# Expert rows gathered in quarters and turned by VectorE in 32x32 blocks, instead of turned by TensorE

## The reference

```python
xf = rms_norm(h, w)                       # (1024, 1024)
logits = xf @ router_w + router_b         # 32 experts
top_logit, top_idx = lax.top_k(logits, 4)
gate = jax.nn.softmax(top_logit, axis=-1)
...
gu = x_blk @ w_gate_up[e] + b_gate_up[e]  # (rows, 2048)
g = jnp.minimum(gu[:, :1024], 7.0)
u = jnp.clip(gu[:, 1024:], -7.0, 7.0)
act = (u + 1.0) * (g * jax.nn.sigmoid(1.702 * g))
yb = act @ w_down[e] + b_down[e]          # added at the rows' tokens, times the gate
```

## Time and profile before

| | |
|---|---|
| median of 3 runs | 2207.5 us (2200.51 to 2211.68) |
| profiled execution | 2205.89 us, span 2204.2 us, mean granted clock 0.989 |
| busy over the span | PE 2130.6 us (97%), PEld 1655.0 (75%), DVE 1569.1 (71%), ACT 1324.6 (60%), POOL 581.7 (26%) |
| experts stage | from 832.31 us (first product) to the end |

### The profile page before, as it was taken

How to read it: one execution, slowest core, us unless ns; L and a number is a source line. 1 busy time by engine, 2 the same in 40 slices (tenths; PEclk the granted TensorE clock), 3 DMA queues, 4 the chain that set the end, 5 groups by cost and what they waited for, 6 DMA issues and landing times.

```text
span 2204.2 us, 38936 instructions
## 1 busy us (share of the span) xinstructions
PE 2130.6 (97%) x13778; PEld 1655.0 (75%) x13779; DVE 1569.1 (71%) x1479; ACT 1324.6 (60%) x1496; POOL 581.7 (26%) x556
## 2 busy tenths in 40 slices
PE   7989999999999989999999999999999999999997
PEld 7867777777777766777777777877887777777775
DVE  4165767676576457787787787787987777767776
ACT  4266666757454225576676675776876566565665
POOL 1120101010075343153353331232331222122222
PEclk9999999999999988999999999999999999999999
DMA  4101212121256539899899898999998898887993
GB/s 153 36 23 47 68 37 69 36 62 56 82 193 199 178 126 357 302 327 347 312 338 350 313 343 283 373 348 345 390 374 314 283 317 327 297 307 266 331 327 112
DMA packets 267125, 515.15 MB, mean 234 GB/s; under 512 B 34821, under 2 KB 77264, under 8 KB 267052
## 3 DMA queue, kind: packets, MB, share of 16 engines
q1 hardware_dynamic: 243052, 471.90, 59.5%
q0 software_dynamic: 17088, 39.14, 7.0%
q10 hardware_dynamic: 6912, 3.15, 0.5%
HBM read 475.82 MB, written 42.45 MB: 235 GB/s over the span
## 4 chain that ended last, share of the span: by engine, by line
PE 59%; SPq 1%; DMA 1%; issue 1%; DVE 0%; ACT 0%; POOL 0%; ACTq 0%; POOLq 0%; DVEq 0%
PE ex_gu L2431 31%; PE ex_yp L2475 15%; PE ex_rest L2453 6%; PE ex_rest L2492 3%; PE ex_gu L2383 1%; SPq L1360 1%; PE ex_tr L2391 1%; PE ex_gu L2391 1%; DMA ex_bias<-bp_s 1%; PE ex_gu L2418 0%; PE ex_tr L2383 0%; PE ex_yp L2422 0%; DVE ex_wlo L2302 0%; ACT ex_whi L2027 0%; PE ex_rest L2447 0%
## 5 line engine op out<-in xcount | busy, mean ns | idle before, releaser
L2302 DVE TENSOR_TENSOR ex_wlo<-ex_raw,ex_whi 128x2048 fp32r<-128x2048 f32 x387 | 873.9, 2291 | 216.5 <-ACT ex_whi L2027 187.3
L2027 ACT ACTIVATE ex_whi<-ex_raw 128x2048 fp32r<-128x2048 f32 x387 | 733.9, 1927 | 176.5 <-PE ex_gu L2431 126.1
L2431 PE MATMUL ex_gu<-ex_whi,ex_xhi 128*128 128x512 f32 x1024 | 284.6, 400 | 1.0 <-DVE ex_xlo L2341 1.0
L2431 PE MATMUL ex_gu<-ex_whi,ex_xlo 128*128 128x512 f32 x1024 | 274.9, 390 | 0.0
L2431 PE MATMUL ex_gu<-ex_wlo,ex_xhi 128*128 128x512 f32 x1024 | 274.9, 390 | 0.0
L2431 PEld LDWEIGHTS ex_gu<-ex_whi,ex_xhi 128*128 128x128 f32 x1024 | 186.8, 189 | 57.1 <-issue 20.6
L2431 PEld LDWEIGHTS ex_gu<-ex_whi,ex_xlo 128*128 128x128 f32 x1024 | 192.8, 188 | 41.1
L2431 PEld LDWEIGHTS ex_gu<-ex_wlo,ex_xhi 128*128 128x128 f32 x1024 | 192.8, 188 | 40.7
L57 PE MATMUL at_job<-xnT_hi,at_whi 128*128 128x512 f32 x416 | 178.4, 429 | 5.3 <-DVE at_nxt_qa L777 2.9
L59 PE MATMUL at_job<-xnT_hi,at_wlo 128*128 128x512 f32 x416 | 164.2, 395 | 0.0
L58 PE MATMUL at_job<-xnT_lo,at_whi 128*128 128x512 f32 x416 | 163.4, 393 | 0.0
(11 more groups left out here) (379 smaller groups left out, 3563.5 us busy)
## 6 DMA issues: line engine op xcount, KB each, us to landing
ex_raw<-in_w_gate_up_dram SPq DMA_DIRECT2D x512, 512.0 KB
ex_raw<-in_w_down_dram SPq DMA_DIRECT2D x256, 512.0 KB
at_raw<-in_w_in_dram SPq DMA_DIRECT2D x25, 512.0 KB
gT<-at_gst SPq DMA_DIRECT2D x32, 256.0 KB, 2.4
mg_g<-gT SPq DMA_DIRECT2D x32, 256.0 KB, 3.8
raw_o<-in_w_out_dram SPq DMA_DIRECT2D x8, 512.0 KB, 5.7
op_x<-in_x_dram SPq DMA_DIRECT2D x8, 512.0 KB, 4.0
out_dram<-op_h SPq DMA_DIRECT2D x8, 512.0 KB, 2.9
```

What stands on the lines that cost most here:

```text
L2027: nc.scalar.activation(w_hi[:, i % RING, :], raw[:, i % SLABS, :], ACT.Copy).then_inc(hi_d, 1)
L2302: nc.vector.tensor_tensor(w_lo[:, slot, :], raw[:, i % SLABS, :], w_hi[:, slot, :].bitcast(F32), ALU.subtract).then_inc(lo_d, 1)
L2431: mm = nc.tensor.matmul(gu[:, half, h, :], x[:, k, :], w[:, kk, h, :], start=half == 0 and k == 0 and n == 0, stop=k == KD - 1 and n == 2)
```

## The change

The normalized rows are stored in `xn_s` with their columns permuted: four quarters of 256 values, of which quarter q holds of each group of 128 columns the 32 columns q*32 to q*32+31. Five indirect DMAs fetch 128 quarters each (4 for the block's 128 rows, 1 for the rest's 32). So partition 32*q+i of piece a holds quarter q of row 32*a+i, and a transpose in 32x32 blocks, which VectorE has, gives the transposed tile. VectorE does this in three instructions in each block, into the hidden tile's buffer (`x_t`), half the columns ahead of the hidden's second lo part together with the rest, half behind it. ScalarE's hi copies and VectorE's lo subtractions read this buffer in place of PSUM; ScalarE's copy of the rest goes. `turn_x` leaves TensorE's queue, which then waits for x by `take_x` as before. The table of tokens gets a form in quarters (`rows_of`), for which TensorE turns 16 small pieces at the stage's start, and VectorE and GpSimd do some more small steps. `normalize` is four instructions in place of one. For blocks not in the table on the chip, GpSimd loads the numbers with 25 DMAs in place of 5 (this happens twice, at the end). The weights' loads keep their order.

```diff
@@ normalize, in output_and_route
-                    nc.vector.scalar_tensor_tensor(out=xn[:, s, :], in0=ht[:, s, :], scalar=rstd[:, t:t + 1],
-                                                   in1=wB[:, :], op0=ALU.mult, op1=ALU.mult).then_inc(xn_done, 1)
+                    piece = lambda b, q: b.rearrange("p (k q c) -> p q k c", k=KD, q=Q)[:, q, :, :]
+                    for q in range(Q):
+                        last = nc.vector.scalar_tensor_tensor(
+                            out=xn[:, s, q * XW:(q + 1) * XW].rearrange("p (k c) -> p k c", k=KD), in0=piece(ht[:, s, :], q),
+                            scalar=rstd[:, t:t + 1], in1=piece(wB[:, :], q), op0=ALU.mult, op1=ALU.mult)
+                    last.then_inc(xn_done, 1)
@@ SyncE, start of experts
-            sp.wait_ge(x_in, 32)
+            for s, n in landed:
+                sp.wait_ge(s, n)
             load(4, 0)
@@ ScalarE, take_x
-                    act.wait_ge(raw_mm, SLABS * (b - 1) + 8)
-                for g in range(3):
-                    act.wait_ge(x_tr, 3 * b + g + 1)
-                    if g < 2:
-                        dst, src = x_hi[:, 4 * g:4 * g + 4, :], gu[:, 0, g, :].rearrange("p (k c) -> p k c", k=4)
-                    else:
-                        dst = x_rest[:, :, :].rearrange("p (q h) c -> p h q c", h=2)
-                        src = tr[:, 0:2 * P].rearrange("p (h q c) -> p h q c", h=2, q=Q)
-                    nc.scalar.activation(dst, src, ACT.Copy).then_inc(xh_d, 1)
+                for g in range(2):
+                    mine = slice(4 * g, 4 * g + 4)
+                    act.wait_ge(x_tr, 2 if isinstance(b, int) and b == 0 else 3 * b + 1 + 2 * g)
+                    nc.scalar.activation(x_hi[:, mine, :], x_t[:, mine, :], ACT.Copy).then_inc(xh_d, 1)
@@ GpSimd, load_slots and gather
+                    for a in range(NQ):
+                        pool.dma_start(nxt_q[q * CAP2:(q + 1) * CAP2, a, :],
+                                       slots[bass.ds(b * CAP + a * CAP2, CAP2), :]).then_inc(idx_in, 16)
...
-            def gather():
-                pool.indirect_dma_start(out=xg[:, :], out_offset=None, in_=xn_s[:, :],
-                                        in_offset=bass.IndirectOffsetOnAxis(ap=nxt[:, 0, 0:1].bitcast(U32), axis=0))\
-                    .then_inc(x_in, 16)
-                pool.indirect_dma_start(out=xg2[:, :], out_offset=None, in_=xn_s.rearrange("t (q c) -> (t q) c", q=Q),
-                                        in_offset=bass.IndirectOffsetOnAxis(ap=idx2[:, 0:1], axis=0)).then_inc(x_in, 16)
+            def gather(table):
+                for a in range(NQ):
+                    pool.indirect_dma_start(out=xg[:, a, :], out_offset=None, in_=xn_s.rearrange("t (q c) -> (t q) c", q=Q),
+                                            in_offset=bass.IndirectOffsetOnAxis(ap=table(a), axis=0)).then_inc(x_in[max(a - 1, 0)], 16)
@@ VectorE
+            def turn_x(b, g):
+                if g == 0:
+                    for s, n in landed:
+                        dve.wait_ge(s, n * (b + 1))
+                after(dve, h_tr, 3 * b + g - 2)
+                mine = slice(4 * g, 4 * g + 4)
+                nc.vector.transpose(x_t[:, mine, :].rearrange("p k (a c) -> p k a c", a=Q),
+                                    pieces[:, mine, 0:Q, :]).then_inc(x_tr, 1)
+
+            def turn_x_rest(b):
+                if not isinstance(b, int) or b > 0:
+                    dve.wait_ge(raw_mm, SLABS * (b - 1) + 8)
+                nc.vector.transpose(x_rest[:, :, :], pieces[:, :, Q, :]).then_inc(x_tr, 1)
...
                 split_lo(b, 11)
+                turn_x(b + 1, 0)
+                turn_x_rest(b + 1)
                 hidden_lo(b, 1)
+                turn_x(b + 1, 1)
                 take_x(b + 1)
@@ VectorE, start of experts
+            for a in range(Q):
+                dve.wait_ge(*landed[max(a - 1, 0)])
+                last = nc.vector.transpose(x_t[:, :, a * CAP2:(a + 1) * CAP2], pieces[:, :, a, :])
+            last.then_inc(x_tr, 2)
             take_x(0)
+            dve.wait_ge(*landed[Q - 1])
+            turn_x_rest(0)
@@ TensorE
                 if more:
                     turn_hidden_rest(b)
-                turn_x(b + 1)
                 main(10)
...
+            for a in range(Q):
+                for q in range(Q):
+                    last = nc.tensor.matmul(turned_q[q * CAP2:(q + 1) * CAP2, a, :], rt["table"][:, a * CAP2:(a + 1) * CAP2],
+                                            rt["pair_sum"][:, 0:NE], start=True, stop=True)
             last.then_inc(t_tr, 1)
-            pe.wait_ge(tab_d, 2)
-            turn_x(0)
```

More of the change, by code:

```diff
@@ L1894, in experts @@
         one_col = sb("ex_one", [P, 1])
-        over_n, cum, base1 = (sb(f"ex_{n}", [P, NE]) for n in ("over", "cum", "base1"))
-        home, low, destf = (sb(f"ex_{n}", [P, NT * TOPK]) for n in ("home", "low", "destf"))
+        over_n, cum, base1, home, low, destf = (rt["table"][:, n * NE:(n + 1) * NE] for n in range(6))
         tabf = sb("ex_tabf", [1, MAXOVER + 1])
@@ L1939, in experts @@
         y_ev, y2_ev = sem("e_y_ev"), sem("e_y2_ev")
-        idx_in, idx2_d, x_in, y_out = sem("idx_in"), sem("idx2_d"), sem("x_in"), sem("e_y_out")
-        mid_d, cur_d, piece_d = sem("e_mid"), sem("e_cur"), sem("e_piece")
+        idx_in, idx_d, x_in, y_out = sem("idx_in"), sem("idx_d"), [sem(f"x_in{n}") for n in range(NQ - 1)], sem("e_y_out")
+        landed = [(x_in[n], 32 if n == 0 else 16) for n in range(NQ - 1)]
+        cur_d = sem("e_cur")
         ones_d, bias_in = sem("e_ones"), [sem(f"e_bias_in{n}") for n in range(2)]
@@ L2155, in next_rows @@
             def next_rows(b, on_chip=True):
-                if not isinstance(b, int) or b > 0:
-                    hold(pool, x_in, 32 * b, spare)
-                    nc.gpsimd.tensor_copy(mid[:, :, :], nxt[:, :, :]).then_inc(mid_d, 1)
-                    hold(pool, mid_d, b, spare)
+                for s, n in landed:
+                    hold(pool, s, n * b, spare)
+                nc.gpsimd.tensor_copy(mid[:, :, :], nxt[:, :, :]).then_inc(idx_d, 1)
+                hold(pool, idx_d, 3 * b - 2, spare)
                 if on_chip:
@@ L2166, in next_rows @@
                     load_slots(b)
-                    hold(pool, idx_in, 16 * (1 + Q) * (b - NE + 1), spare)
-                rows()
-                hold(pool, idx2_d, b + 1, spare)
-                if not isinstance(b, int) or b > 0:
-                    hold(pool, x_tr, 3 * b, spare)
-                gather()
+                    hold(pool, idx_in, 16 * (1 + Q * (1 + NQ)) * (b - NE + 1), spare)
+                    nc.gpsimd.tensor_scalar(idx[:, :], nxt_q[:, :, 0].bitcast(U32), float(Q), quarter[:, 0:1],
+                                            ALU.mult, ALU.add).then_inc(idx_d, 1)
+                hold(pool, idx_d, 3 * b - 1, spare)
+                hold(pool, x_tr, 3 * b, spare)
+                gather(lambda a: idx[:, a:a + 1])
             def first_rows():
@@ L2217, in body @@
                     scatter(t)
-                hold(pool, piece_d, b + 1, spare)
+                hold(pool, idx_d, 3 * b + 3, spare)
                 if isinstance(b, int) and b == NE - 2:
@@ L2374, in _ @@
             pe.sem_inc(slab_mm, RING)
-            def turn_x(b):
-                pe.wait_ge(x_in, 32 * b + 32)
-                for g in range(3):
-                    dst = gu[:, 0, g, :] if g < 2 else tr[:, :]
-                    for k in range(4 if g < 2 else 2):
-                        src = xg[:, (4 * g + k) * P:(4 * g + k + 1) * P] if g < 2 else xg2[:, k * P:(k + 1) * P]
-                        last = nc.tensor.transpose(dst[:, k * P:(k + 1) * P], src, ident[:, :])
-                    last.then_inc(x_tr, 1)
             def turn_hidden(b, half, alone=False):
@@ L2526, in _ @@
             for h in range(2):
-                last = nc.tensor.matmul(tr[:, 2 * NE * h:2 * NE * (h + 1)], rt["table"][:, h * P:(h + 1) * P],
-                                        rt["pair_sum"][:, :], start=True, stop=True)
+                nc.tensor.matmul(tr[:, 6 * NE * h:6 * NE * h + 2 * NE], rt["table"][:, h * P:(h + 1) * P],
+                                 rt["pair_sum"][:, :], start=True, stop=True)
+            for a in range(Q):
+                for q in range(Q):
+                    last = nc.tensor.matmul(turned_q[q * CAP2:(q + 1) * CAP2, a, :], rt["table"][:, a * CAP2:(a + 1) * CAP2],
+                                            rt["pair_sum"][:, 0:NE], start=True, stop=True)
             last.then_inc(t_tr, 1)
-            pe.wait_ge(tab_d, 2)
-            turn_x(0)
             def body(b, over):
```

66 lines of the change are left out of this document (40 added, 26 removed).

## The result

The changed kernel took 2225.19 us (median of 4 runs, 2222.6 to 2227.06), the kernel before 2206.07 beside it (2200.51 to 2211.68): a ratio of 1.0086, 95% interval 1.0057 to 1.0114. The forecast was 2203.9 with a range up to 2220, so it is outside. The profiled span grew from 2204.2 to 2224.0 us.

| stretch, us of the profiled span | before | changed | changed, tiles moved back |
|---|---|---|---|
| up to the first gather | 823.72 | 825.47 | 825.32 |
| first gather to slab 0 | 8.59 | 12.01 | 11.96 |
| 32 blocks | 1357.19 | 1361.12 | 1354.12 |
| last product to the end | 14.74 | 25.43 | 21.74 |

A forecast was written before the change was run, and what follows sets the result against it. TensorE was taken to bound the experts stage. 7.4 us less in the blocks against 3.8 us added at single places gave net -3.6: 2202.3 for the profiled execution, 2203.9 as median, range 2194 to 2220.

The forecast's parts named there:

- rival 3: Short blocks: VectorE's transpose costs a multiple of its plain rows and VectorE becomes the bound; 2217 at twice; chance 0.14.
- rival 4: Gathers: 1 KB pieces not packed, 480 more packets and 4.5 us more DMA a block; 2220; chance 0.07.
- What was removed, and what it covered: Ahead of slab 10: removed transposes covered a wait for ScalarE's copy; gain 0.34 us a long block, 0.13 a short one.
- Rival 2: All blocks: TensorE goes on at 0.44, all 36 us saved less 3.8, 2175; chance 0.11 together with gains in between.
- The four behind another short one: Short blocks following another short one: VectorE's loop about as long as TensorE's was, so they gain nothing.
- 7.4 of the blocks: Experts stage: 18 long blocks at 0.34 plus 10 short ones at 0.13, 7.4 us less.
- Start, forecast +1.7: Before slab 0: table from small products and five gathers, the fourth gating x; slab 0 +1.95 later, taken as +1.7 us.
- End, forecast +0.9: After the last block: ScalarE's slab copies end later, +0.7; GpSimd's 25 loads instead of 5 and three more gathers, +0.2.
- Third block, forecast +1.0: Third block: VectorE is already behind, so its 0.97 us of transposes is exposed, +1.0.
- The bias wait, forecast +0.2: Behind the run of four short blocks: the one wait for biases takes back what the run's first block gained, +0.2.
- the steps to slab 0: Start: fourth gather lands at 831.9, then transpose 0.42, two copies 1.1, subtraction 0.7; slab 0 at about 834.25.

The follow-up runs named there:

- changed, tiles moved back: Changed kernel, its four small route tiles packed in one plus an unused 64-byte tile, so weight tiles lie as before; no instruction changed: 2212.57 us, 1.0034.
- run 1: Kernel before, with 7 of the 10 x transposes of each block after the first left out on TensorE and nothing put in their place: 2201.04 us, 0.997.
- run 7: Two edits on "changed, tiles moved back": VectorE's first weight subtraction behind the start's x transposes and subtractions, 2211.7 us; bias load one slab earlier, 2214.23 us.
- Run 3: Changed kernel, with the 20 small quarter-table loads for blocks past the last expert made 4 (9 loads instead of 25): 2217.48 us, 1.0053.
- e_five_back: Kernel before with rows fetched in five gathers, its three new small index tiles placed behind all others so older tiles keep their places: 2207.69 us, 1.001.
- run 6: Kernel before with only tiles shifted; here all tiles of the experts' stage 64 bytes later, no instruction changed: 2211.17 us, 1.0027.
- e_bias: "changed, tiles moved back" with the bias load ahead of slab 8's weight load instead of slab 9's: 2214.23 us, 1.0043.
- e_tail: Same as Run 3: changed kernel with 9 loads instead of 25 for each block past the last expert: 2217.48 us, 1.0053.
- p_before_96: Kernel before with an unused 96-byte tile ahead of x_hi, shifting x_hi and all tiles behind it; no instruction changed: 2233.25 us, 1.0124.
- p_before_64: Kernel before with the weight tiles 64 bytes later, everything from the bias tile on at its old place; no instruction changed: 2217.05 us, 1.005.
- p_x_minus64: Kernel before with the x tiles and all else behind the small tables 64 bytes earlier, weights in place; no instruction changed: 2211.22 us, 1.0034.

## Why the prediction was wrong

**How far off.** The profiled span was to shrink by 3.6 us and grew by 19.8, a miss of 23.4: 10.1 of it in the blocks (-6.2 forecast, +3.9 measured), 9.8 at the end (+0.9, +10.7) and 3.5 at the start (+1.7, +5.2). The prediction gave "slower by over 0.5%" a chance of 0.21, for rivals 3 and 4; it came out slower, but by neither.

**What was removed, and what it covered.** Right, to the hundredth once the tiles are back: -0.35 a long block (forecast 0.34), -0.10 to -0.15 for nine short ones behind a long one (the tenth is the third block). The four behind another short one gained 0.06 to 0.09 where nothing was forecast. Rival 2 is excluded by run 1 and by the wait of 18.0 us.

**The step that failed first is one the prediction doesn't have.** It costed each instruction that is added or moved and took the new tiles at nothing. Moving the weight tiles by 64 bytes against the x tiles made the products' spacing 1.7 ns longer (229.1 against 227.4); for 3072 products in the gate and up slabs and at 1.2 ns more for 1536 in the down slabs that is 7.1 us, and 7.0 were measured between slab 0 and the last product (1361.12 against 1354.12). That eats nearly the whole 7.4 of the blocks. The other 3.1 us that the blocks missed by are the third block's and the bias wait's, below. In medians the tiles are worth 12.6 us; the other 3.7 us of the span lie at the end, on GpSimd, where steps differ by some us between executions, so only the 7.0 are shown to be the spacing's.

**Start, forecast +1.7.** Slab 0 came 5.17 later. Of this 1.75 lies ahead of the first gather, most of it in the route stage, whose end varies in these 17 traces between 813.8 and 820.0 us. The rest, 3.42, is a term that was mis-sized: the first gather was taken at 1.25 and took 3.89, since the change also drops VectorE's wait for GpSimd's first tables and its subtraction now runs beside the gather (run 7: 1.26 without it). With the tiles back block 0 took 49.75 us instead of 50.40, 0.3 more than a long block's gain; the prediction had allowed 0.25 for this.
The Trainium skill (SBUF — State Buffer, "SBUF: two separate sides") calls the port pair that VectorE and GpSimd share an exclusive lock, taken by a VectorE operation with two SBUF inputs against a GpSimd operation that reads SBUF, and says that whichever starts first has it for the whole instruction. These traces agree that the two collide, with 3.89 against 1.26 us, and with gathers in the changed kernel at 2.06 us on average beside such a subtraction and 1.32 otherwise. They don't show that order: the gather had started 0.50 us ahead of the subtraction and was still the one that grew, while the subtraction took its usual 2.27 us.

**End, forecast +0.9: the largest single term that was mis-sized.** +10.7 in the trace. The loads were counted rightly (25, ten us more), but they were set in a wait of 11 us while the steps around them were taken at their old durations: cur and piece took 2.01 and 2.07 instead of 0.19 and 0.26, the landing 3.37, the index 4.38 instead of 0.26. Run 3 takes back 7.7.

**Third block, forecast +1.0.** +1.73, and +1.75 with the tiles back. At slab 10 the forecast holds: there the subtraction ends 3.77 behind the start of the hidden transposes and the pass starts at 3.82, where it was 2.91 before. The rest stands at the block's start, in a term the prediction doesn't have: TensorE waits 1.10 us for ScalarE's copy of the results instead of 0.28.

**The bias wait, forecast +0.2.** Behind the run of four short blocks the changed kernel waits 3.0 us in block 19 (put down to "issue", ahead of the product that needs the bias) and the one with moved-back tiles 2.5 us in block 20, against 1.2 before. The wait costs more than itself: in the changed kernel the granted clock is 1.00 up to 1634 us and then, behind the wait,

```profile
1637.00:1638.00 1.00, 1.00 (x7) 0.20 (x7) 1.00 (x2) 0.00 (x0) 1.00 (x1) 0.51 1.00 389
```

The clock is the third figure from the end, 0.51. So block 19 took 4.8 us longer than before, and block 20 of the moved-back kernel 2.5, although before it held a wait too. That one, of 1.2 us, had left the clock at 1.00. The five gathers alone leave it at 1.7 us (e_five_back), and a mere shift of all tiles makes it 4.2 (run 6), so the gathers alone don't set its size; the load's place in its queue does (e_bias).

**DMA, rivals 3 and 4.** VectorE's transposes took 0.70 and 0.40 us, so rival 3 is out. GpSimd's queue has 20000 packets instead of 17088 for the same bytes in the whole kernel. The gathers make 1584 of these 2912 (e_five_back has 18672), some 50 a block where rival 4 wanted 480, and nearly all the rest are the small loads at the end (18976 in e_tail, with 32 of them gone). Run e_five_back prices the gathers at 2.6 us at most: rival 4 is out.

**Sums of the prediction that don't come out**, without weight for the result: by its own terms the short block's subtraction starts at 1.58 and ends at 2.27, so TensorE could go on at 2.33 and nothing of the cover was left (the trace has the low half at 2.04); the steps to slab 0 add up to 834.1, not 834.25; and at twice the transposes' price the low half comes at 3.4, not 3.0.

What stays open is why a distance sets the spacing. 0 bytes (as before) gives 227.4, -64 gives 229.1, +32 and +64 give 233.2, +96 gives 234.2 ns; moving both sides by 64 gives 227.7. Which of the tiles behind x_hi matters wasn't tried, nor other distances. What makes the "issue" wait ahead of slab 0 come and go is open too.

## What to carry to other kernels

Before costing a change's instructions, list where its new tiles push the old ones; a kernel bound by TensorE can be tested for this with an unused tile, and any comparison of two versions should hold the operands' places fixed. An instruction that goes from the bounding engine is worth only what the engine doesn't then wait for: find what it covered, and move other work into its place in the same edit. At a kernel's end, count an engine's chain with the durations it has beside a busy neighbour, and take small loads out of it.

## What was not expected of the hardware

The place of operands in SBUF, by 32 to 96 bytes and with no instruction changed, moved TensorE's spacing between 227.4 and 234.2 ns and the 32 blocks of a 2205 us kernel by up to 25.6 us (p_before_96, 28 us slower in all). An "issue" wait of 5 us ahead of slab 0 came and went between kernels with the same instructions (5.5 us in p_before_64, none in p_x_minus64). GpSimd's copy of 128x4 elements took from 0.19 to 2.34 us, its index step from 0.26 to 4.38, where VectorE's subtractions of two SBUF tiles ran beside them; with none beside, no such copy in these traces took over 0.7 us. The weight subtractions themselves took 2.25 to 2.35 us throughout. A wait of TensorE of 3.0 us in the blocks was followed by products at a granted clock of 0.50, one of 1.2 wasn't.
